# Attention probabilities of two mixers: crossed by DMA in 16-bit halves instead of turned on TensorE

## What is computed

```python
def dsa_mixer(h, w_in, q_g, k_g, w_out):            # mixer a; moba_mixer (b) is the same without the selection
    q, k, v, gate, qi, ki, wi = split_cols(h @ w_in, A_WIDTHS)
    q = rope(rms_norm(q.reshape(B, T, N_HEADS, HEAD_DIM), q_g), pos)
    k = rope(rms_norm(k.reshape(B, T, N_KV_HEADS, HEAD_DIM), k_g), pos)
    ...
    logits = jnp.einsum('bqgrd,bqkgd->bqgrk', qb, k_sel) * scale
    logits = jnp.where(valid[:, :, None, None, :], logits, NEG)
    p = jax.nn.softmax(logits, axis=-1)
    o = jnp.einsum('bqgrk,bqkgd->bqgrd', p, v_sel)
    return (jax.nn.silu(gate) * o) @ w_out
```

## Time and profile before

| | us |
|---|---|
| median of 3 runs | 2264.7 (2264.47 to 2265.18) |
| profiled execution | 2264.24 |
| its span on the core | 2262.9 |
| PE busy | 2241.5 (99%) |
| DVE busy | 1367.7 (60%) |
| ACT busy | 1226.0 (54%) |
| transposes L539, matmul rows, a, b and c | 23.8 in 144 |

### The profile page before, as it was taken

The page is one execution under the profiler, slowest core; times in us unless marked ns, Lnnn a source line. Parts: engine busy times, 40 slices in busy tenths (PEclk is TensorE's granted clock), DMA queues, the critical chain, the costliest instruction groups (busy, mean ns, idle before and its releaser), DMA issues.

```text
span 2262.9 us, 28305 instructions
## 1 busy us (share of the span) xinstructions
PE 2241.5 (99%) x11586; PEld 1850.2 (82%) x11586; DVE 1367.7 (60%) x1860; ACT 1226.0 (54%) x1670; POOL 9.6 (0%) x17
## 2 busy tenths in 40 slices
PE   9999999999999999999999999999999999999998
PEld 7888888888888888888788888888888888888886
DVE  5776665756665676575765556665555455554555
ACT  5556675656675664464554555565544344544444
POOL 0000000000000000000000000000000000000000
PEclk9999999999999999999999999999999999999999
DMA  8454557654557654444644446677666666656663
GB/s 274 146 186 149 159 178 226 204 193 152 179 172 229 191 167 132 148 132 156 217 149 149 156 161 209 209 224 217 213 202 196 198 200 197 214 193 188 201 206 112
DMA packets 275809, 417.83 MB, mean 185 GB/s; under 512 B 83488, under 2 KB 83648, under 8 KB 275552
## 3 DMA queue, kind: packets, MB, share of 16 engines
q1 hardware_dynamic: 273520, 408.91, 56.7%
q0 software_dynamic: 1584, 6.16, 0.9%
q10 hardware_dynamic: 576, 0.95, 0.1%
HBM read 396.06 MB, written 2.10 MB: 176 GB/s over the span
## 4 chain that ended last, share of the span: by engine, by line
PE 94%; ACT 2%; DVE 2%; DMA 1%; issue 1%; SPq 0%; DVEq 0%; ACTq 0%
PE ACC L959 29%; PE ACC L961 28%; PE ACC L960 28%; ACT arena L988 1%; PE TP L539 1%; PE SCPV L531 1%; DMA W<-in_a_w_in 1%; ACT WH L988 1%; DVE WL L2021 1%; PE SCPV L548 0%; PE SCPV L549 0%; PE SCPV L547 0%; PE SCPV L530 0%; PE TP L519 0%; PE SCPV L696 0%
## 5 line engine op out<-in xcount | busy, mean ns | idle before, releaser
L2021 DVE TENSOR_TENSOR WL<-W,WH 128x1024 fp32r<-128x1024 f32 x740 | 901.0, 1219 | 642.1 <-ACT WH L988 640.8
L988 ACT ACTIVATE WH<-W 128x1024 fp32r<-128x1024 f32 x740 | 781.1, 1056 | 807.5 <-PE ACC L961 800.6
L959 PE MATMUL ACC<-WH,XH 128*128 128x512 f32 x2592 | 1036.8, 400 | 3.3 <-ACT arena L988 2.0
L961 PE MATMUL ACC<-WH,XL 128*128 128x512 f32 x2592 | 1011.3, 390 | 0.0
L960 PE MATMUL ACC<-WL,XH 128*128 128x512 f32 x2592 | 1009.5, 389 | 0.0
L959 PEld LDWEIGHTS ACC<-WH,XH 128*128 128x128 f32 x2592 | 487.0, 188 | 111.3 <-issue 4.9
L961 PEld LDWEIGHTS ACC<-WH,XL 128*128 128x128 f32 x2592 | 486.5, 188 | 104.2
L960 PEld LDWEIGHTS ACC<-WL,XH 128*128 128x128 f32 x2592 | 487.5, 188 | 95.0 <-issue 1.0
L959 PE MATMUL ACC<-WH,HH 128*128 128x512 f32 x328 | 128.8, 393 | 0.0
L961 PE MATMUL ACC<-WH,HL 128*128 128x512 f32 x328 | 127.7, 389 | 0.0
L960 PE MATMUL ACC<-WL,HH 128*128 128x512 f32 x328 | 127.7, 389 | 0.0
(11 more groups left out here) (293 smaller groups left out, 1288.8 us busy)
## 6 DMA issues: line engine op xcount, KB each, us to landing
W<-in_w_in SPq DMA_DIRECT2D x84, 1024.0 KB, 5.0
W<-in_a_w_in SPq DMA_DIRECT2D x47, 1024.0 KB, 5.1
W<-in_w_ffn_gate SPq DMA_DIRECT2D x44, 1024.0 KB, 5.2
W<-in_w_ffn_up SPq DMA_DIRECT2D x44, 1024.0 KB, 5.2
W<-in_w_ffn_down SPq DMA_DIRECT2D x44, 1024.0 KB, 5.0
W<-in_b_w_in SPq DMA_DIRECT2D x40, 1024.0 KB, 5.1
W<-in_a_w_out SPq DMA_DIRECT2D x16, 1024.0 KB, 5.5
W<-in_b_w_out SPq DMA_DIRECT2D x16, 1024.0 KB, 5.5
```

The lines of the kernel that those rows point to most:

```text
L959: MM(out, hx, WH[:, k, 0:ch.width], start=q == 0 and k == 0, stop=False)
L961: ins = MM(out, lx, WH[:, k, 0:ch.width], start=False, stop=last and k == QK - 1)
L988: return nc.scalar.activation(out, in_, func, **how)
L2021: TT(tiles_of(M.WL[K.pair(n)], ch, half), tiles_of(M.W[n % 4], ch, half), tiles_of(M.WH[K.pair(n)], ch, half).bitcast(F32), ALU.subtract). ...
```

## The change

- The three transposes per head on PE, and ACT's copy of them out of TP, are gone in a and b (32 heads). Mixer c keeps its `heads_attended`.
- Two heads (a pair p) are crossed at a time: PR[0] and PR[1] lie side by side as 768 words. ACT copies the low halves, DVE the high ones, to `PROB_HALVES`; SP crosses them (`cross_probs`); ACT and DVE join them in the place of PT.
- PE's scores stay where they were. The output products of both heads of a pair stand at s+15 and s+16 (pair 0) and s+21 and s+22 (pair 1), where before they stood at s+9, s+12, s+15 and s+18.
- DVE's loop counts from s: split at s+8 and s+14, join at s+14 and s+20. ACT's loop starts at offset 2 in step s+3, so its labels stand one visit later: exponentials at s+5+3h as before, split at s+9 and s+15, join at s+15 and s+21, `store` at s+16, s+17, s+22, s+23.
- SP's crossings are sorted by visit in front of the weight DMA that follows.
- The joined tiles of the gated outputs 0 and 3 move from 16640 to 4096 in the arena, since 16640 now holds the halves, and two waits on that place go.

```diff
+PROBS_SPLIT, PROBS_JOINED = 8, 14
 def sp_program(K):
+    def cross_probs(l, g, p):
+        sp.wait_ge(*at("low_prob_halves", l, g, p))
+        sp.wait_ge(*at("high_prob_halves", l, g, p))
+        sp.dma_start_transpose(M.PROBS_CROSSED, M.PROB_HALVES.rearrange("p u w -> p (u w)")).then_inc(*did("probs_crossed", l, g, p, by=16))
...
+            if name == "attend":
+                for p in range(GRP // 2):
+                    at_visit = visit + PROBS_SPLIT + 6 * p
+                    crossings.setdefault((at_visit + 1) // 4 + 5, []).append((at_visit, cross_probs, args + [p]))
 def pe_program(K):
-        yield from heads_attended(l, g, QT, PT, lambda t0, n: M.KT[:, g, t0:t0 + n], lambda t: M.V[:, t, g * HD:(g + 1) * HD])
+        for offset in range(3, PROBS_JOINED + 9):
+            h, rest = divmod(offset - 3, 3)
+            if h < GRP and rest == 0:
...
+            p, rest = divmod(offset - PROBS_JOINED - 1, 6)
+            if 0 <= p < GRP // 2 and rest < 2:
+                h, b = 2 * p + rest, rest
+                wait_empty(f"PV{b}")
+                pe.wait_ge(*at("low_probs_joined", l, g, p))
+                pe.wait_ge(*at("high_probs_joined", l, g, p))
+                MM(PV[b][:, 0:HD], PT[b][:, 0:P], v(0), start=True, stop=True)
...
+            yield
 def act_program(K):
-        yield from heads_attended(l, g, M.att, store)
+        for offset in range(2, PROBS_JOINED + 9):
+            p, rest = divmod(offset - PROBS_JOINED, 6)
+            if 0 <= p < GRP // 2 and rest == 0:
+                act.wait_ge(*at("probs_crossed", l, g, p))
...
+                A(M.PROBS_TURNED.bitcast(U16).rearrange("p (n u) -> p n u", u=2)[:, :, 0], M.PROBS_CROSSED[:, 0:6, :].rearrange("p n q -> p (n q)"), ACT.Copy).then_inc(
+                    *did("low_probs_joined", l, g, p))
+            if 0 <= p < GRP // 2 and rest in (1, 2):
+                store(2 * p + rest - 1)
+            p, rest = divmod(offset - PROBS_SPLIT, 6)
+            if 0 <= p < GRP // 2 and rest == 0:
+                act.wait_ge(*at("probs_exponentiated", l, g, 2 * p + 1))
...
+                A(M.PROB_HALVES[:, 0, :], M.PROBS.bitcast(U16).rearrange("p (w u) -> p w u", u=2)[:, :, 0], ACT.Copy).then_inc(*did("low_prob_halves", l, g, p))
+            h, rest = divmod(offset - 4, 3)
+            if 0 <= h < GRP and rest == 0:
...
 def dve_program(K):
+        for offset in range(PROBS_JOINED + 7):
+            p, rest = divmod(offset - PROBS_JOINED, 6)
+            if 0 <= p < GRP // 2 and rest == 0:
+                dve.wait_ge(*at("probs_crossed", l, g, p))
...
+                V.tensor_copy(M.PROBS_TURNED.bitcast(U16).rearrange("p (n u) -> p n u", u=2)[:, :, 1], M.PROBS_CROSSED[:, 6:12, :].rearrange("p n q -> p (n q)")).then_inc(
+                    *did("high_probs_joined", l, g, p))
+            p, rest = divmod(offset - PROBS_SPLIT, 6)
+            if 0 <= p < GRP // 2 and rest == 0:
+                dve.wait_ge(*at("probs_exponentiated", l, g, 2 * p + 1))
...
+                V.tensor_copy(M.PROB_HALVES[:, 1, :], M.PROBS.bitcast(U16).rearrange("p (w u) -> p w u", u=2)[:, :, 1]).then_inc(*did("high_prob_halves", l, g, p))
```

More of the change, by code:

```diff
@@ L398, in memory @@
     M.GBS, M.CS = cut(22690, TB, HQ), cut(22698, TB * HQ)
+    M.PROBS, M.PROBS_TURNED = cut(13312 + 1792, 6 * P), cut(13312 + 2560, 6 * P)
+    M.PROB_HALVES = cut(16640, 6 * P).bitcast(U16).rearrange("p (u w) -> p u w", u=2)
+    M.PROBS_CROSSED = cut(16640 + 6 * P, 6 * P).bitcast(U16).rearrange("p (n q) -> p n q", q=P)
     pair = lambda at: (cut(at, 1024), cut(at + 1024, 1024))
@@ L412, in memory @@
     M.CROSSED = {l: r[1].bitcast(U16).rearrange("p (n q) -> p n q", q=P) for l, r in rooms.items()}
-    M.JOINED = {"go": [cut(at, QK, T) for at in (16640, 11264, 12288, 16640)], "x": [cut(at, QK, T) for at in (16640, 11264, 13312, 14336)],
+    M.JOINED = {"go": [cut(at, QK, T) for at in (4096, 11264, 12288, 4096)], "x": [cut(at, QK, T) for at in (16640, 11264, 13312, 14336)],
                 "mx": [cut(at, QK, T) for at in (4096, 5120, 6144, 4096)], "x.d": [cut(at, QK, T) for at in (5120, 6144, 4096, 5120)],
@@ L436, in sp_program @@
             if name == "halves":
-                crossings.setdefault((visit + 1) // 4 + 5, []).append(args)
+                crossings.setdefault((visit + 1) // 4 + 5, []).append((visit, cross, args))
+            if name == "attend":
+                for p in range(GRP // 2):
+                    at_visit = visit + PROBS_SPLIT + 6 * p
+                    crossings.setdefault((at_visit + 1) // 4 + 5, []).append((at_visit, cross_probs, args + [p]))
     for ch in K.chunks:
@@ L440, in sp_program @@
             n = ch.first + q
-            for args in crossings.get(n, ()):
-                cross(*args)
+            for _, crossing, args in sorted(crossings.get(n, ()), key=lambda c: c[0]):
+                crossing(*args)
             if n < NC_D:
@@ L564, in attend @@
         pe.wait_ge(*at("keys_turned", l, 1))
-        yield from heads_attended(l, g, QT, PT, lambda t0, n: M.KT[:, g, t0:t0 + n], lambda t: M.V[:, t, g * HD:(g + 1) * HD])
+        v = lambda t: M.V[:, t, g * HD:(g + 1) * HD]
+        for offset in range(3, PROBS_JOINED + 9):
+            h, rest = divmod(offset - 3, 3)
+            if h < GRP and rest == 0:
+                b = h % 2
+                wait_empty(f"SC{b}")
+                MM(SC[b][:, 0:P], QT[:, h, 0:P], M.KT[:, g, 0:P], start=True, stop=True)
+                MM(SC[b][:, P:3 * P], QT[:, h, P:T], M.KT[:, g, 0:T], start=True, stop=True).then_inc(*did("scores_multiplied", l, g, h))
+                emptied[f"SC{b}"] = ("scores_masked", l, g, h)
+            p, rest = divmod(offset - PROBS_JOINED - 1, 6)
[5 more added lines that the diff above has]
+                MM(PV[b][:, 0:HD], PT[b][:, 0:P], v(0), start=True, stop=True)
+                MM(PV[b][:, HD:2 * HD], PT[b][:, P:2 * P], v(0), start=True, stop=False)
+                MM(PV[b][:, HD:2 * HD], PT[b][:, 2 * P:3 * P], v(1), start=False, stop=True).then_inc(*did("outputs_multiplied", l, g, h))
+                emptied[f"PV{b}"] = ("outputs_taken", l, g, h)
+            yield
     def index():
@@ L1121, in store @@
             A(M.Q[:, 1, c:c + HD], PV[h % 2][:, HD:2 * HD], ACT.Copy, scale=M.SUM[:, h, 1:2]).then_inc(*did("outputs_taken", l, g, h))
-        yield from heads_attended(l, g, M.att, store)
+        QT, LG, PR, PT = M.att
+        for offset in range(2, PROBS_JOINED + 9):
+            p, rest = divmod(offset - PROBS_JOINED, 6)
+            if 0 <= p < GRP // 2 and rest == 0:
+                act.wait_ge(*at("probs_crossed", l, g, p))
+                if p:
+                    act.wait_ge(*at("outputs_multiplied", l, g, 2 * p - 1))
+                elif g:
+                    act.wait_ge(*at("outputs_multiplied", l, g - 1, GRP - 1))
+                A(M.PROBS_TURNED.bitcast(U16).rearrange("p (n u) -> p n u", u=2)[:, :, 0], M.PROBS_CROSSED[:, 0:6, :].rearrange("p n q -> p (n q)"), ACT.Copy).then_inc(
[5 more added lines that the diff above has]
+                act.wait_ge(*at("probs_exponentiated", l, g, 2 * p + 1))
+                if p:
+                    act.wait_ge(*at("probs_crossed", l, g, p - 1))
+                elif g:
+                    act.wait_ge(*at("probs_crossed", l, g - 1, GRP // 2 - 1))
+                A(M.PROB_HALVES[:, 0, :], M.PROBS.bitcast(U16).rearrange("p (w u) -> p w u", u=2)[:, :, 0], ACT.Copy).then_inc(*did("low_prob_halves", l, g, p))
+            h, rest = divmod(offset - 4, 3)
+            if 0 <= h < GRP and rest == 0:
+                b = h % 2
+                table_of(ACT.Exp)
+                act.wait_ge(*at("scores_topped", l, g, h))
+                if h >= 2:
+                    act.wait_ge(*at("high_prob_halves", l, g, 0))
+                    act.wait_ge(*at("low_prob_halves", l, g, 0))
+                elif g:
+                    act.wait_ge(*at("high_prob_halves", l, g - 1, 1))
+                    act.wait_ge(*at("low_prob_halves", l, g - 1, 1))
+                A(PR[b][:, 0:P], LG[b][:, 0:P], ACT.Exp, bias=M.NM[:, h, 0:1], accum_out=M.SUM[:, h, 0:1])
+                A(PR[b][:, P:3 * P], LG[b][:, P:3 * P], ACT.Exp, bias=M.NM[:, h, 1:2], accum_out=M.SUM[:, h, 1:2]).then_inc(*did("probs_exponentiated", l, g, h))
+            yield
     def index():
@@ L1601, in attend @@
     def attend(l, g):
[L1602 to L1607, removed]
+        QT, LG, PR, PT = M.att
+        mask, rq = M.MASK if l == "a" else M.causal, M.rq[g % 2]
+        for offset in range(PROBS_JOINED + 7):
+            p, rest = divmod(offset - PROBS_JOINED, 6)
+            if 0 <= p < GRP // 2 and rest == 0:
+                dve.wait_ge(*at("probs_crossed", l, g, p))
+                if p:
+                    dve.wait_ge(*at("outputs_multiplied", l, g, 2 * p - 1))
+                elif g:
+                    dve.wait_ge(*at("outputs_multiplied", l, g - 1, GRP - 1))
```

(29 more changed lines are left out.)

## The result

The changed kernel takes 2279.98 us (2279.82 to 2280.14, four runs) against 2264.59 for the kernel before beside it: a ratio of 1.0068, with a 95% interval of 1.0053 to 1.0083. It is 15.4 us slower; the forecast was 2272, in a range up to 2278. Its profiled execution took 2279.82 us.

What follows compares the result with a forecast made beforehand. PE, busy for 99% of the span, was taken to bound the kernel. From 2264.24 us, a gain of 15.9 and new waits of 23.6 gave 2271.9, 2272.4 from the median; forecast 2272 (2269 to 2276), range 2260 to 2278.

Steps and rivals of the forecast that it cites:

- Removed from PE: Transposes of 32 heads in mixers a and b go from PE, 0.33 us each: 10.6 us gained.
- waits removed: PE's waits for exponentials before the transposes in a and b go: 5.3 us, the middle of 3.7 and 6.9.
- The new wait: PE's output products wait for joined tiles, as ACT's labels run one visit late: 23.6 us (21 to 26).
- pair 1 of groups 2 and 3: ACT's join follows a rounding that waits for PE: 1.15 us each, four times in a and b, 4.6 us.
- the join of 1.0 us: Time of ACT's join of 768 elements, taken as 1.0 us (0.84 to 1.10).
- Pair 0 of groups 0 and 1: PE waits for rounding, head 3's exponentials, then ACT's join: 0.69 us each, four times, 2.8 us.
- E(s+13): Start of PE's last matmul of visit s+13, for which ACT's rounding waits in pair 0 of groups 0 and 1.
- Beside these, at nothing: Added copies on DVE and ACT and crossings on SP are covered by other work and cost nothing.
- the third rival: Crossings on the DMA queue land 1 to 2 us later each, 16 us on top: about 2285; chance 0.06.
- granted clock at full: Sign expected in the profile after: PE's clock does not fall, so the forecast adds nothing for it.
- Rival 4: PE's clock falls in four waits of 3 us and more, 5.6 us on top: 2278; chance 0.06.
- Rivals 1 and 2: 1: join in time, nothing lost, 2249, chance 0.14; 2: waits of 11 to 20 us, 2260 to 2269, chance 0.20.

Runs made afterwards that it cites:

- experiment 1: Kernel before with the three transposes per head left out in mixers a and b, ACT copying unturned probabilities, nothing put in their place: 2248.94 us (the floor).
- experiment 3: Changed kernel with ACT's join alone issued one visit earlier: 2257.41 us (2255.93 to 2259.07).
- experiment 7: Changed kernel with ACT's join one visit earlier, output products and stores one visit later (two in group 2 of mixer a): 2248.88 us, ratio 0.9932.
- experiment 2: Changed kernel with PE's output products and ACT's stores one visit later, joins left where they were: 2257.68 us (2256.12 to 2260.95).
- experiment 4: Changed kernel with extra PE products that nobody reads filling three long waits of pair 0: 2275.28 us; filling all four: 2273.81 us.

## Why the prediction was wrong, point by point

- **Removed from PE, 10.6 us, and waits removed, 5.3 us: right as a sum.** Together 15.9, measured 15.4 (experiment 1). Only the sum is measured; how it divides between the two, no run shows.
- **The new wait: right in kind, place and sum.** 14 of 16 places wait; the formula for pair 1 of groups 2 and 3 gave 1.15 and the trace 1.03; the join of 1.0 us is 1.05 on average. All places together are 25.1 for 23.6, inside the stated 21 to 26. That the sum agrees is partly luck: pair 0 of groups 0 and 1 came out 3.2 us longer, the other places 1.7 shorter. In two of the 14 places DVE's join ended last, not ACT's. With a join of 0.83 the prediction's own terms give 23.6 - 14 x 0.17 = 21.2, not a sum below 21; measured, the join took 1.05.
- **Pair 0 of groups 0 and 1: mis-sized.** The term of 0.69 each, 2.8 us for four, measured 1.4 and 1.6, 6.0 for four. The step that was too short is "the rounding waits for E(s+13), then head 3's exponentials". It let the exponentials follow the rounding at once and took DVE as in time in these places. In group 1, DVE first makes a rest that waits for ACT's rounding at 214.68, and head 3's masking and maxima stand behind that rest:

```profile
215.75 1.23 DVE L2120 TENSOR_TENSOR WL<-W,WH 128x1024 fp32r<-128x1024 f32 x1 [0.79 <-ACT WH L1021]
...
217.87 0.41 DVE L1701 TENSOR_REDUCE maxima<-arena 128x1 f32<-128x256 f32 x1
```
```profile
214.68 1.04 ACT L1021 ACTIVATE WH<-W 128x1024 fp32r<-128x1024 f32 x1
216.26 1.06 ACT L1021 ACTIVATE WH<-W 128x1024 fp32r<-128x1024 f32 x1 [0.55 <-PE ACC L994]
218.32 0.40 ACT L1021 ACTIVATE arena<-arena,maxima 128x128 f32<-128x128 f32 x1 [0.99 <-DVE maxima L1701]
```

  So ACT's exponentials began 218.32 - 216.26 - 0.97 = 1.1 us later than I let them. In group 0 they waited 0.48 for maxima, and the rotation of the next group's queries stands ahead of DVE's join, which ended 1.39 us after PE's last matmul began, 0.2 after ACT's (experiment 3). This step accounts for 3.2 us.
- **Beside these, at nothing: right.** Experiment 7 has all of it and stands at the floor. Crossings of 3.6 to 4.8 us, not 4.3 to 5.2, were in time in the changed kernel; the third rival doesn't occur. DVE's joins took 0.60, a little over the "at most 0.57".
- **The clock: the step that failed.** The forecast's sum put the clock at nothing ("granted clock at full"), and it fell three times, for 5.7 us. Rival 4 had the right mechanism. Its size, 5.6 us, is right partly by luck: it took 1.4 each for four falls, and there were three, at 1.32, 1.59 and 2.84. But the rival got a chance of 0.06, because no wait of that length stood in the trace. That was no evidence against it: the forecast itself put four waits of 3 us and more into PE, and the only row after an idle stretch showed the low pace. What followed from the forecast should have gone into it. 2272 + 5.7 for the clock + 1.5 for the waits = 2279.2; the gain, 0.5 smaller than forecast, makes most of the rest to 2279.98. The upper end of the range had the clock without the waits' own upper end, 26, and so ended at 2278. The rule cited beside it, from the Trainium skill's "TensorE: Matmul & The Clock Gate", section "Why this matters for your kernels", is borne out in mid-kernel by the rows above, with falls behind waits of 3.96, 3.00 and 3.00 us; in experiments 2 and 4 falls came behind waits of 2.61 and 2.48 too.
- **Rivals 1 and 2: wrong for this order.** The 2249 of rival 1 is what experiment 7 gives in another order: the crossing pays as soon as every join is done before it is asked for.

The account closes: 2248.9 (floor) + 25.1 (waits) + 5.7 (clock) = 2279.7, beside 2279.82 for the profiled execution.

## What to carry to other kernels

When work moves from the engine that sets the time to one that has time over, check in which step each engine meets it: here a label that stood one visit late on ACT alone made 22.6 of the 30.8 us between a gain of 15.4 and a loss of 15.4. Follow the queue in front of the new step on the slower engine back to whatever it waits for, on every engine it passes through. If a forecast puts waits of some 3 us on TensorE, add the fall of its clock to the same forecast, and once the waits are gone, look for the next deadline that they had covered, here the eviction of a full bank.

## What the runs showed of the hardware beyond that

- The granted clock fell in mid-kernel behind PE waits of 3.96, 3.00 and 3.00 us in the changed kernel (the mean over the run was 0.995 or 0.996 in all four runs, where the kernel before has 0.999). Behind waits of 2.5 to 2.7 us it went either way: one of 2.49 was followed by full clock in the changed kernel and one of 2.48 in the same place by a fall in experiment 4. The runs of experiment 3, whose longest wait is 2.72, differ by some 3 us: 2255.93 and 2256.02 at a mean granted clock of 0.999, 2258.70 and 2259.07 at 0.998. Where the clock was low in the latter isn't shown, as the profiled run is the one of 2256.02. A fall cost 1.3 to 2.8 us beside the wait. PE matmuls of the main work then stand 0.43 us apart instead of 0.23. The last rows on it are of experiment 2, PE in order of time, behind the wait of 2.61 us:

```profile
262.02 0.46 PE L594 MATMUL SCPV<-arena 128*128 128x128 f32 x2 [2.45 <-ACT arena L1021]
...
263.00 0.63 PE L993 MATMUL ACC<-WL,XH 128*128 128x512 f32 x1
263.43 0.63 PE L994 MATMUL ACC<-WH,XL 128*128 128x512 f32 x1
```

  The first matmuls behind that wait still ran at the full pace; the granted clock was 1.00 up to 262.9 and 0.50 from 263.0 on, 1.0 us after PE had started again. In groups 2 and 3 of mixer a in the changed kernel it had fallen while PE still waited (a mean of 0.56 from 265.5 to 266.0, PE from 266.14; 0.52 from 309.9 to 310.7, PE from 310.70).
- Extra products that nobody reads, issued in front of four waits that had to be served anyway, made the changed kernel 5.9 us faster (2279.98 to 2273.81, each less the kernel before beside it).
- A copy of 768 16-bit words on ACT takes 0.83 us when it reads interleaved and writes densely, 1.05 us when it writes interleaved. On DVE the two are 0.55 and 0.60.
